# Turning the gated activations by 32 x 32 VectorE transposes and SBUF to SBUF transfers instead of on TensorE

## The chip, the cores and the metric

The kernel runs on one core of a Trainium2 chip. The metric is the device time of one execution in microseconds (us), as a median over runs. The core has five engines that run their own instruction streams in order and meet only through semaphores: TensorE (PE), which multiplies and turns matrices, VectorE (DVE), ScalarE (ACT), GpSimd (POOL) and SyncE (SP), which here issues the weight loads. A transfer can be issued from SP, from ACT or from POOL; the issue is an instruction in that engine's stream.

## The reference

Two transformer blocks in sequence over 256 tokens of width 1024, all in float32. The first has differential attention, retention and a squared-relu feed-forward of width 4096. The second has two gated feed-forwards ("f1" and "f2") of width 2816, one ahead of its attention and one behind it. Only these two are touched:

```
def swiglu(x, w_gate, w_up, w_down):
    return (jax.nn.silu(x @ w_gate) * (x @ w_up)) @ w_down
...
        x = x + FFN_RES * swiglu(rms_norm_2(x, ffn1_norm[l]), ffn1_w_gate[l], ffn1_w_up[l], ffn1_w_down[l])
...
        x = x + FFN_RES * swiglu(rms_norm_2(x, ffn2_norm[l]), ffn2_w_gate[l], ffn2_w_up[l], ffn2_w_down[l])
```

## The kernel before, in words

Weights come from HBM in units of 128 x 2048 float32 (1 MB), issued by SP into six `raw` slots. Every product is made of three: each weight is cut into a high part `w_hi` (ACT, a rounding copy, function `hi`) and a low part `w_lo` (DVE, a subtraction, `lo`, written over the raw slot), and each activation likewise into a `hi` and a `lo` tile. TensorE adds hi by hi, hi by lo and lo by hi.

A gated feed-forward (`gated`, one function of that name per engine) walks over 11 blocks of 256 columns of the 2816, numbered 0 to 10. A step i takes three weight units: v and v+1 hold gate and up columns of block i, v+2 holds the down rows of block i-1. On TensorE the step is: `ff_up` with unit v for both halves of the tokens (tb 0 and 1); `ff_turn`, four 128 x 128 transposes that turn the activation of block i-1 from tokens by columns to columns by tokens, into PSUM; `ff_up` with unit v+1; then `down`, 24 matmuls that multiply the turned block i-1 by unit v+2. Block 0 is done ahead of step 1, steps 2 to 9 stand in a loop of two rounds over four, step 10 is written out behind it with the turns of block 10.

ACT in a step: `hi(v+3)`, two `split` copies of the turned block from PSUM into `fT_hi`, `hi(v+4)`, `silu` for both token halves, `hi(v+5)`. DVE in a step: `lo(v+3)`, two `split` subtractions into `fT_lo`, `lo(v+4)`, two `multiply` (silu times up, into `act_f`), `lo(v+5)`. `hi(u)` waits until unit u-4 is used (four `w_hi` slots), `lo(u)` waits for `hi(u)`, `silu` for its half of `ff_up`, `multiply` for `silu`, `ff_turn` for `multiply`, and `down` for the `split`. The order of each engine's instructions is the order in which the code is written; no scheduler moves them.

Of the kernel before, what the change touches and what calls it, by code (L numbers as in the profile page):

```python
# [28 lines left out]
P = 128  # L29
D, TB, SEQ = 1024, 2, 256  # L30
# [5 lines left out]
HALF = 512  # L36
# [60 lines left out]
def work_batches():  # L97

    order = [("mix", 0, 0), ("mix", 1, 0), ("mix", 0, 1), ("mix", 1, 1)]
    for k in range(IN_CB):  # L100
        if k == 1:
            order += [("qk", 0, tb) for tb in range(TB)]
        if 6 <= k < 14:
            order += [("a", k - 6), ("v", k - 6)]
        if k == IN_CB - 1:
            order += [("ya", 0, 0)]
        if 12 <= k:
            order += [("rv", k - 12)]
    order += [("ya", 0, 1)]
    order += [("ya", 1, h) for h in range(2)]  # L110
    order += [("yr", tb, h) for tb in range(TB) for h in range(2)]
    order += [("m", tb, h) for tb in range(TB) for h in range(2)]
    order += [("mlp", tb, h) for tb in range(TB) for h in range(2)]
    order += [("p",)]
    order += [("ff", 0, tb) for tb in range(TB)]
    order += [("ple", tb, h) for tb in range(TB) for h in range(2)]
    order += [("ffn1", tb, h) for tb in range(TB) for h in range(2)]
    order += [("f1", i, tb) for i in range(FF2 // SUB) for tb in range(TB)]
    order += [("mix2", tb, h) for tb in range(TB) for h in range(2)]
    order += [("mq", tb) for tb in range(TB)] + [("cq", 0), ("cq", 1), ("ckv",)] + [("mk", tb) for tb in range(TB)]  # L120
    for kind in "bl":
        for j in range(BH // 2):
            order += [(kind + "a", 2 * j), (kind + "a", 2 * j + 1)]
            order += [(kind + "v", j)]
    order += [("ffn2", tb, h) for tb in range(TB) for h in range(2)]
    order += [("f2", i, tb) for i in range(FF2 // SUB) for tb in range(TB)]
    return {name: n for n, name in enumerate(order)}
# [38 lines left out]


# [17 lines left out]
def two_blocks(nc, x_d, p_d, g_mix, w_in, lam_q1, lam_k1, lam_q2, lam_k2, g_diff, g_ret, w_bd, w_br, w_out,  # L185
# [85 lines left out]
    fT, pT, fE = [fT0, fT1], [pT0, pT1], [fE0, fE1]  # L271
    (mix_t,) = lay(named["va"], ("mix_t", [P, TB, D]))
# [66 lines left out]
    f_hi, f_ready = sem("f_hi"), sem("f_ready")  # L339
    up_done, act_ready, up_out = sem("up_done"), sem("act_ready"), sem("up_out")  # L340
# [160 lines left out]
    def _(pe):  # L501
# [302 lines left out]
        def ff_up(u, name, i, steps, cols, du=0, di=0):  # L804

            for j in range(2):
# [7 lines left out]
                if j == 0:  # L814
                    ff_turn(name, i - 1, 2 * steps, cols, di)
# [97 lines left out]
        def gated(name, norm, base):  # L913
# [5 lines left out]
            def down(v, i, tb, r=0, first=False, last=False):  # L919

                turned((name, i, tb), 4 * r)
# [13 lines left out]
            with pe.Fori(0, 2) as r:  # L935
# [5 lines left out]
            narrow_block(up(0)[:, :], None, v, 0, HALF, lambda: ff_turn(name, i - 1, 2 * (base + i), SUB))\  # L941
                .then_inc(up_done, 1)
# [8 lines left out]
            else:  # L951
                turned((name, i - 1, 1))
# [165 lines left out]
    def _(act):  # L1118
# [268 lines left out]
        def gated(name, norm, base):  # L1387
# [6 lines left out]

            silu(0, 0)
# [3 lines left out]
            def step(i, r=0):  # L1399
                v = u + 2 + 3 * (i - 1)  # L1400
                hi(v + 3, r)
                for tb in range(TB):
                    split((name, i - 1, tb), 4 * r)
                hi(v + 4, r)
# [8 lines left out]
            for tb in range(TB):  # L1413
                split((name, i - 1, tb))
            hi(v + 3)
            silu(i, 0)
# [141 lines left out]
    def _(vec):  # L1558
# [343 lines left out]
        def gated(name, norm_in, base, norm_out):  # L1902
# [8 lines left out]

            multiply(0, 0)
# [423 lines left out]
```

## Time and profile before

| | |
|---|---|
| median of three runs | 988.9 us (988.61 to 989.17) |
| the profiled execution's own time | 988.44 us |
| its span in the profile | 986.6 us |
| granted TensorE clock | 1.00 of full speed |
| busy share of PE, PEld, DVE, ACT, POOL | 99, 83, 60, 51, 7 per cent |
| span of the two gated feed-forwards | about 507 to 676 us and about 808 to 977 us |

The span is the time from the first to the last instruction on the core. PE is the matmul side of TensorE, PEld its weight loads (of the stationary operand), which run beside it. Busy shares count neither the issuing of transfers nor waits.

### The profile page before, as it was taken

The page shows a single profiled execution, that of the slowest core. Times are in us where ns is not written, and L with a number is a line of the kernel's source. Part 1 is how long each engine was busy: PE and PEld are TensorE (multiplying, and loading weights), DVE is VectorE, ACT ScalarE, POOL GpSimd, SP SyncE. Part 2 cuts the span into 40 slices and gives each one's busy share as a digit, 9 for nine tenths or more (in the row PEclk, how much of TensorE's full clock was granted, in tenths as well). Part 3 has the DMA queues.
Part 4 walks back from the last instruction along what each step waited for, and adds up shares of the span by engine and source line. Part 5 has one row for each costly group of instructions (what it writes and reads, how often), then busy time and mean ns, then how long its engine had stood idle before and what let it go on. Part 6 is the DMA issues. An engine that isn't in the chain of part 4 may idle for free.

```text
span 986.6 us, 13371 instructions
## 1 busy us (share of the span) xinstructions
PE 979.5 (99%) x5000; PEld 822.5 (83%) x5000; DVE 594.9 (60%) x847; ACT 499.8 (51%) x707; POOL 65.9 (7%) x97
## 2 busy tenths in 40 slices
PE   9999999999999999999999999999999999999997
PEld 7989888888889888888888888888887788888886
DVE  6646655478666555665775545446658875455544
ACT  7444555744365444444684444435648674343433
POOL 4101000020020000000120000000203020000000
PEclk9999999999999999999999999999999999999999
DMA  9754554434465655555566555544654256556531
GB/s 344 254 178 164 171 171 162 154 129 171 171 220 202 195 189 191 193 185 167 177 212 206 178 186 197 174 145 135 217 177 145 86 173 194 189 177 206 172 126 43
DMA packets 98726, 175.71 MB, mean 178 GB/s; under 512 B 5920, under 2 KB 54128, under 8 KB 98672
## 3 DMA queue, kind: packets, MB, share of 16 engines
q1 hardware_dynamic: 97024, 171.53, 51.6%
q0 software_dynamic: 1344, 3.19, 1.2%
q8 instruction: 35, 0.57, 0.2%
q10 hardware_dynamic: 304, 0.27, 0.1%
q14 instruction: 19, 0.16, 0.0%
HBM read 173.91 MB, written 1.05 MB: 177 GB/s over the span
## 4 chain that ended last, share of the span: by engine, by line
PE 99%; issue 0%; DVE 0%; ACT 0%; POOL 0%; POOLq 0%; ACTq 0%
PE bank L523 76%; PE bank L644 6%; PE bank L857 5%; PE bank L537 4%; PE bank L862 2%; PE bank L836 1%; PE bank L582 1%; PE bank L581 1%; PE bank L593 1%; PE bank L994 1%; PE bank L678 0%; PE bank L1056 0%; PE bank L595 0%; PE bank L594 0%; PE bank L613 0%
## 5 line engine op out<-in xcount | busy, mean ns | idle before, releaser
L1573 DVE TENSOR_TENSOR w_lo<-raw,w_hi 128x2048 fp32r<-128x2048 f32 (+1 forms) x159 | 359.3, 2265 | 222.6 <-ACT w_hi L1131 222.4
L523 PE MATMUL bank<-w_hi,hA 128*128 128x512 f32 (+1 forms) x1368 | 431.5, 392 | 0.0
L1131 ACT ACTIVATE w_hi<-raw 128x2048 fp32r<-128x2048 f32 (+1 forms) x162 | 306.0, 1893 | 178.0 <-PE bank L523 133.1
L523 PEld LDWEIGHTS bank<-w_hi,hA 128*128 128x128 f32 x1368 | 255.4, 188 | 51.5 <-issue 0.6
L523 PE MATMUL bank<-w_lo,hA 128*128 128x512 f32 (+1 forms) x684 | 259.8, 387 | 0.0
L523 PEld LDWEIGHTS bank<-w_lo,hA 128*128 128x128 f32 x684 | 128.6, 188 | 25.0
L523 PE MATMUL bank<-w_hi,fT_hi 128*128 128x512 f32 x232 | 71.8, 391 | 0.0
L523 PE MATMUL bank<-w_hi,fT_lo 128*128 128x512 f32 x232 | 71.5, 389 | 0.0
L523 PE MATMUL bank<-w_lo,fT_hi 128*128 128x512 f32 x232 | 71.5, 389 | 0.0
L1138 ACT ACTIVATE fT_hi<-bank 128x256 fp32r<-128x256 f32 (+1 forms) x46 | 15.9, 391 | 86.2 <-PE bank L537 86.2
L644 PE MATMUL bank<-hA,w_hi 128*128 128x256 f32 x320 | 58.2, 284 | 0.0
L857 PE MATMUL bank<-hA,w_hi 128*128 128x512 f32 x192 | 52.3, 394 | 0.0
L523 PEld LDWEIGHTS bank<-w_lo,fT_hi 128*128 128x128 f32 x232 | 43.5, 188 | 9.2
L523 PEld LDWEIGHTS bank<-w_hi,fT_lo 128*128 128x128 f32 x232 | 43.5, 188 | 9.1
L644 PEld LDWEIGHTS bank<-hA,w_hi 128*128 128x128 f32 x320 | 49.8, 192 | 0.6 <-ACT va L1183 0.3
L523 PEld LDWEIGHTS bank<-w_hi,fT_hi 128*128 128x128 f32 x232 | 43.0, 188 | 8.7 <-issue 0.2
L2190 POOL TENSOR_SCALAR ms<-ss 128x1 f32<-128x1 f32 x15 | 9.4, 626 | 609.0 <-ACT junk L1161 608.7
L1392 ACT ACTIVATE act_r<-bank,rs 128x256 f32<-128x256 f32 x44 | 20.9, 475 | 53.9 <-PE bank L523 52.2
L1592 DVE TENSOR_TENSOR fT_lo<-bank,fT_hi 128x256 fp32r<-128x256 f32 (+1 forms) x46 | 18.1, 432 | 45.1 <-ACT fT_hi L1138 45.1
L644 PE MATMUL bank<-hA,w_lo 128*128 128x256 f32 x160 | 45.3, 283 | 0.0
L857 PEld LDWEIGHTS bank<-hA,w_hi 128*128 128x128 f32 x192 | 33.2, 189 | 4.8
L1600 DVE SCALAR_TENSOR_TENSOR hA<-bank,g_col,hA 128x128 fp32r<-128x128 f32 x92 | 25.3, 343 | 16.6 <-ACT hA L1143 16.4
(306 smaller groups left out, 1086.0 us busy)
## 6 DMA issues: line engine op xcount, KB each, us to landing
raw<-in_w_in SPq DMA_DIRECT2D x74, 512.0 KB, 4.5
raw<-in_w_ff SPq DMA_DIRECT2D x64, 512.0 KB, 4.3
raw<-in_ffn_w_gate SPq DMA_DIRECT2D x44, 512.0 KB, 3.8
raw<-in_ffn_w_up SPq DMA_DIRECT2D x44, 512.0 KB, 4.8
raw<-in_ffn_w_down SPq DMA_DIRECT2D x44, 512.0 KB, 4.0
raw<-in_w_out SPq DMA_DIRECT2D x16, 512.0 KB, 4.2
raw<-in_w_branch_diff SPq DMA_DIRECT2D x8, 512.0 KB, 4.3
raw<-in_w_branch_ret SPq DMA_DIRECT2D x8, 512.0 KB, 4.3
```

The lines of the kernel that those rows point to most:

```text
L523: mm = pe.matmul(o, a, w, start=first and t == 0 and m < len(outs), stop=last and t == n - 1 and m >= len(todo) - len(outs))
L537: mm = pe.transpose(work(name)[0:cols, col:col + rows], blk, ident)
L581: pe.matmul(b[:, 0:P], q[:, h, 0:P], k[:, h, 0:P], start=True, stop=True)
L644: mm = pe.matmul(out, w, a[:, kt, :], start=(j, f % 2, t, m) == (0, 0, 0, 0), stop=(j, t, m) == (1, 3, 2), skip_group_check=True)
L857: pe.matmul(out[:, :], hi, hA_both[:, kt, :, :], start=(j, t) == (0, 0), stop=(j, t) == (1, 3), skip_group_check=True)
L862: mm = pe.matmul(out[:, 0:SEQ], lo, hA[0][:, kt, :], start=False, stop=(j, t) == (1, 3), skip_group_check=True)
L1131: act.activation(w_hi[u % HI_SLOTS][:, 0:w], raw[u % RAW_SLOTS][:, 0:w], ACT.Copy).then_inc(hi_ready, 1)
L1138: act.activation(dst, b, ACT.Copy).then_inc(split_hi, 1)
L1392: act.activation(act_r[:, tb, 0:SUB], up(tb, i)[:, 0:SUB], ACT.Silu, scale=inv_rms(norm, tb))\
L1573: vec.tensor_tensor(w_lo[u % RAW_SLOTS][:, 0:w], raw[u % RAW_SLOTS][:, 0:w], w_hi[u % HI_SLOTS][:, 0:w].bitcast(f32), ALU.subtract).then_i ...
L1592: vec.tensor_tensor(dst, b, hi.bitcast(f32), ALU.subtract).then_inc(work_out[WB[name] % 2], 1)
L1600: vec.scalar_tensor_tensor(out=dst[:, n, :], in0=b[:, n, :], scalar=g_col[:, c0 + n:c0 + n + 1], in1=hi[:, n, :].bitcast(f32), op0=ALU.mul ...
```

## The change

Blocks 1 to 9 of both gated feed-forwards are no longer turned on TensorE. DVE turns each token half of `act_f` in squares of 32 x 32 into a tile `act_Q` (`turn_act`, two instructions). ACT then issues sixteen transfers from `act_Q` to `act_T` (`carry`), each 32 partitions by 128 columns (16 KB), which put the squares into the right groups of partitions. `turned_split` (ACT) copies `act_T` into `fT_hi` in one instruction of 128 x 512, `turned_low` (DVE) writes `fT_lo` in one of the same size, where there were two of 128 x 256 each. Blocks 0 and 10 stay as they were.

```
@@ ff_up
-                if j == 0:
+                if j == 0 and i == 1:
                     ff_turn(name, i - 1, 2 * steps, cols, di)
@@ gated, TensorE
-                turned((name, i, tb), 4 * r)
+                if i in (0, n - 1):
+                    turned((name, i, tb))
+                else:
+                    pe.wait_ge(turned_lo, TURNED[name] + i + 4 * r)
...
-            narrow_block(up(0)[:, :], None, v, 0, HALF, lambda: ff_turn(name, i - 1, 2 * (base + i), SUB))\
-                .then_inc(up_done, 1)
+            narrow_block(up(0)[:, :], None, v, 0, HALF).then_inc(up_done, 1)
@@ gated, ScalarE
+            def carry(i, r=0):
+
+                act.wait_ge(act_turned, 2 * (TURNED[name] + i + 4 * r))
+                for a in range(4):
+                    for j in range(4):
+                        act.dma_start(act_T[32 * j:32 * j + 32, a, :], act_Q[32 * a:32 * a + 32, j, :]).then_inc(act_moved, 16)
+
+            def turned_split(i, r=0):
+                act.wait_ge(act_moved, 256 * (TURNED[name] + i + 4 * r))
+                act.activation(fT[0][:, 2 * (i % 2):2 * (i % 2) + 2, :].rearrange("p k (t a c) -> p a (k t) c", a=4, c=32),
+                               act_T[:, :, :].rearrange("p a (n c) -> p a n c", c=32), ACT.Copy).then_inc(turned_hi, 1)
...
-                hi(v + 3, r)
-                for tb in range(TB):
-                    split((name, i - 1, tb), 4 * r)
-                hi(v + 4, r)
+                if i == 1:
+                    hi(v + 3, r)
+                    for tb in range(TB):
+                        split((name, 0, tb))
+                    hi(v + 4, r)
+                else:
+                    carry(i - 1, r)
+                    hi(v + 3, r)
+                    hi(v + 4, r)
+                    turned_split(i - 1, r)
...
-            for tb in range(TB):
-                split((name, i - 1, tb))
+            carry(i - 1)
             hi(v + 3)
+            turned_split(i - 1)
             silu(i, 0)
@@ gated, VectorE
+            def turn_act(i, r=0):
+
+                vec.wait_ge(up_out, 2 * (base + i) + 2 + 8 * r)
+                there = act_Q[:, :, :].rearrange("p j (k t c) -> p t j k c", k=2, c=32)
+                for tb in range(TB):
+                    vec.transpose(there[:, tb], act_f[:, tb, 0:SUB].rearrange("p (k j f) -> p j k f", j=4, f=32)).then_inc(act_turned, 1)
+
+            def turned_low(i, r=0):
+
+                vec.wait_ge(turned_hi, TURNED[name] + i + 4 * r)
+                hi, dst = (t[:, 2 * (i % 2):2 * (i % 2) + 2, :] for t in fT)
...
+                if i > 1:
+                    turn_act(i - 1, r)
                 lo(v + 3, 12 * r)
-                for tb in range(TB):
-                    split((name, i - 1, tb), 4 * r)
+                if i == 1:
+                    for tb in range(TB):
+                        split((name, 0, tb))
                 lo(v + 4, 12 * r)
+                if i > 1:
+                    turned_low(i - 1, r)
...
-            for tb in range(TB):
-                split((name, i - 1, tb))
+            turn_act(i - 1)
+            turned_low(i - 1)
+            multiply(i, 0)
             lo(v + 3)
-            multiply(i, 0)
             split((name, i, 0))
```

ScalarE, step 2 of the first feed-forward, before (L1131 is `hi`, L1138 `split`, L1392 `silu`; ISA and REGISTER_ALU compute the loop's wait values; unit_used counts used weight units, up_done finished halves of `ff_up`):

```order
L1131 ACTIVATE w_hi_83<-raw_75 128x2048 [waits raw_in5]
L1135 ISA
L1138 ACTIVATE fT_hi<-bank 128x2x128 [waits work_done]
L1135 REGISTER_ALU
L1138 ACTIVATE fT_hi<-bank 128x2x128 [waits work_done]
L1128 REGISTER_ALU
L1131 ACTIVATE w_hi_84<-raw_70 128x2048 [waits raw_in0,unit_used]
L1306 REGISTER_ALU
L1392 ACTIVATE act_r<-bank,rs 128x256 [waits rstd_ready,up_done]
```

The same place of the change (L1137 is `hi`, L1406 the transfers of `carry`, L1410 `turned_split`, L1398 `silu`; act_turned is counted up by DVE's transposes, act_moved by the landings):

```order
L1406 DMA act_T<-act_Q 32x128 [waits act_turned]
L1406 DMA act_T<-act_Q 32x128 x15
L1134 ISA
L1135 ISA [waits unit_used]
L1137 ACTIVATE w_hi_83<-raw_75 128x2048 [waits raw_in5]
L1134 REGISTER_ALU
L1137 ACTIVATE w_hi_84<-raw_70 128x2048 [waits raw_in0,unit_used]
L1409 REGISTER_ALU
L1410 ACTIVATE fT_hi<-act_T 128x4x4x32 [waits act_moved]
L1312 REGISTER_ALU
L1398 ACTIVATE act_r<-bank,rs 128x256 [waits rstd_ready,up_done]
```

Sixteen issues now stand at the head of the step, ahead of both `hi`, and the copy into `fT_hi` has moved from between the two `hi` to behind them.

VectorE, the same step, before (L1573 is `lo`, L1592 `split`, L1909 `multiply`):

```order
L1573 TENSOR_TENSOR w_lo_81<-raw_75,w_hi_83 128x2048 [waits hi_ready]
L1591 ISA
L1592 TENSOR_TENSOR fT_lo<-bank,fT_hi 128x2x128 [waits split_hi]
L1591 REGISTER_ALU
L1592 TENSOR_TENSOR fT_lo<-bank,fT_hi 128x2x128 [waits split_hi]
L1571 REGISTER_ALU
L1573 TENSOR_TENSOR w_lo_76<-raw_70,w_hi_84 128x2048 [waits hi_ready]
L1908 ISA
L1909 SCALAR_TENSOR_TENSOR act_f<-bank,rs,act_r 128x256 [waits act_ready]
```

And of the change, from the last `lo` of step 1 on (L1597 is `lo`, L1941 `turn_act`, L1948 `turned_low`, L1933 `multiply`):

```order
L1597 TENSOR_TENSOR w_lo_80<-raw_74,w_hi_82 128x2048 [waits hi_ready]
L1970 UNCONDITIONAL_BRANCH
L1970 ISA
L1941 STREAM_TRANSPOSE act_Q<-act_f 128x8x32 [waits up_out]
L1941 STREAM_TRANSPOSE act_Q<-act_f 128x8x32
L1595 ISA
L1597 TENSOR_TENSOR w_lo_81<-raw_75,w_hi_83 128x2048 [waits hi_ready]
L1595 REGISTER_ALU
L1597 TENSOR_TENSOR w_lo_76<-raw_70,w_hi_84 128x2048 [waits hi_ready]
L1945 ISA
L1948 TENSOR_TENSOR fT_lo<-act_T,fT_hi 128x4x4x32 [waits turned_hi]
```

The transposes stand behind the last `lo` of the step before, and the subtraction into `fT_lo` stands behind both `lo` of its own step. On TensorE the rows of the step are the same but for the four transposes, which are gone; `down` waits for turned_lo, that is, for `turned_low` of the whole block, where it waited for each token half apart.

## Rows read from the trace of the kernel before

**Rows 1.** The page: busy times, and the chain that ended last, by engine.

```profile
PE 979.5 (99%) x5000; PEld 822.5 (83%) x5000; DVE 594.9 (60%) x847; ACT 499.8 (51%) x707; POOL 65.9 (7%) x97
...
PE 99%; issue 0%; DVE 0%; ACT 0%; POOL 0%; POOLq 0%; ACTq 0%
```

**Rows 2.** Windows, step 2 of f1: stretch, length, PE, PEld, DVE, ACT, POOL, clock, DMA share.

```profile
527.80:544.60 16.80, 16.80 (x79) 13.91 (x77) 8.51 (x7) 7.13 (x7) 0.00 (x0) 1.00 0.57 188
```

**Rows 3.** Timeline, PE in step 3: start, length, engine, line, tile.

```profile
543.96 0.39 PE L523 MATMUL bank<-w_hi,hA 128*128 128x512 f32 x1
...
544.19 0.60 PE L537 MATMUL bank<-masks,act_f 128*128 128x128 f32 x4
...
544.86 0.40 PE L523 MATMUL bank<-w_lo,hA 128*128 128x512 f32 x1
...
550.12 0.62 PE L523 MATMUL bank<-w_hi,fT_hi 128*128 128x512 f32 x2
...
555.56 0.39 PE L523 MATMUL bank<-w_hi,hA 128*128 128x512 f32 x1
```

**Rows 4.** Timeline, ACT at the end of step 3.

```profile
550.32 0.47 ACT L1392 ACTIVATE act_r<-bank,rs 128x256 f32<-128x256 f32 x1 [2.25 <-PE bank L523]
550.69 1.91 ACT L1131 ACTIVATE w_hi<-raw 128x2048 fp32r<-128x2048 f32 x1
```

**Rows 5.** Timeline, DVE in steps 1 and 3.

```profile
511.33 4.50 DVE L1573 TENSOR_TENSOR w_lo<-raw,w_hi 128x2048 fp32r<-128x2048 f32 x2 [1.32 <-ACT w_hi L1131]
515.75 0.75 DVE L1592 TENSOR_TENSOR fT_lo<-bank,fT_hi 128x256 fp32r<-128x256 f32 x2
...
518.61 0.87 DVE L1909 SCALAR_TENSOR_TENSOR act_f<-bank,rs,act_r 128x256 f32<-128x256 f32 x2
519.39 2.28 DVE L1573 TENSOR_TENSOR w_lo<-raw,w_hi 128x2048 fp32r<-128x2048 f32 x1
...
552.63 2.29 DVE L1573 TENSOR_TENSOR w_lo<-raw,w_hi 128x2048 fp32r<-128x2048 f32 x1 [1.32 <-ACT w_hi L1131]
```

**Rows 6.** Tiles: 128 x 512 from SBUF on ACT and DVE; a 128 x 256 cast.

```profile
L1323 ACT ACTIVATE fT_hi<-act_f x6: 625/631/637, 333.4 to 422.5; 128x512 fp32r<-128x512 f32 x6
L1847 DVE TENSOR_TENSOR fT_lo<-act_f,fT_hi x6: 684/685/687, 335.8 to 424.9; 128x512 fp32r<-128x512 f32 x6
...
689.16 0.28 DVE L1995 CAST pos_k<-pos_ki 128x256 f32<-128x256 int32 x1
```

**Rows 7.** Timeline, transfer issues of ACT and SP at the start.

```profile
1.21 0.57 ACTq L1218 DMA_DIRECT2D g_rows<-in_g_mix  x1
...
1.18 0.90 SPq L402 DMA_DIRECT2D raw<-in_w_in  x2
2.12 0.43 SPq L395 DMA_DIRECT2D x<-in_x  x1
2.60 0.91 SPq L402 DMA_DIRECT2D raw<-in_w_in  x2
3.54 0.43 SPq L395 DMA_DIRECT2D x<-in_x  x1
4.02 0.43 SPq L402 DMA_DIRECT2D raw<-in_w_in  x1
```

**Rows 8.** Source L376, SP's weight issues: ns least, median, most.

```profile
L376 SPq DMA_DIRECT2D raw<-in_ffn_w_down x44: 328/345/647, 490.7 to 947.2; - x44
```

**Rows 9.** DMA issues: KB each, median us from issue to landing.

```profile
raw<-in_ffn_w_up SPq DMA_DIRECT2D x44, 512.0 KB, 4.8
...
out<-src ACTq DMA_DIRECT2D x1, 192.0 KB, 2.6
...
lam_v<-in_lam_k POOLq DMA_DIRECT2D x2, 32.0 KB, 6.1
```

**Rows 10.** Timeline, PE at `down` of block 1.

```profile
533.30 0.62 PE L523 MATMUL bank<-w_hi,fT_hi 128*128 128x512 f32 x2
```

More of the change, by code:

```diff
@@ L117, in work_batches @@
     order += [("ffn1", tb, h) for tb in range(TB) for h in range(2)]
-    order += [("f1", i, tb) for i in range(FF2 // SUB) for tb in range(TB)]
+    order += [("f1", i, tb) for i in (0, FF2 // SUB - 1) for tb in range(TB)]
     order += [("mix2", tb, h) for tb in range(TB) for h in range(2)]
@@ L125, in work_batches @@
     order += [("ffn2", tb, h) for tb in range(TB) for h in range(2)]
-    order += [("f2", i, tb) for i in range(FF2 // SUB) for tb in range(TB)]
+    order += [("f2", i, tb) for i in (0, FF2 // SUB - 1) for tb in range(TB)]
     return {name: n for n, name in enumerate(order)}
@@ L165 @@
         _n += 1
+TURNED = {"f1": 0, "f2": FF2 // SUB - 2}
 TALL = (1, 2, 3, 6, 7)
@@ L271, in two_blocks @@
     fT, pT, fE = [fT0, fT1], [pT0, pT1], [fE0, fE1]
+    act_Q, act_T = lay(named["fE_lo"] + 16 * SEQ, ("act_Q", [P, 4, P]), ("act_T", [P, 4, P]))
     (mix_t,) = lay(named["va"], ("mix_t", [P, TB, D]))
@@ L339, in two_blocks @@
     f_hi, f_ready = sem("f_hi"), sem("f_ready")
+    act_turned, act_moved, turned_hi, turned_lo = sem("act_turned"), sem("act_moved"), sem("turned_hi"), sem("turned_lo")
     up_done, act_ready, up_out = sem("up_done"), sem("act_ready"), sem("up_out")
@@ L951, in gated @@
             else:
-                turned((name, i - 1, 1))
+                pe.wait_ge(turned_lo, TURNED[name] + i - 1)
                 turned((name, i, 1))
@@ L1910, in multiply @@
                                          in1=act_r[:, tb, 0:SUB], op0=ALU.mult, op1=ALU.mult).then_inc(up_out, 1)
+            def turn_act(i, r=0):
+                vec.wait_ge(up_out, 2 * (base + i) + 2 + 8 * r)
+                there = act_Q[:, :, :].rearrange("p j (k t c) -> p t j k c", k=2, c=32)
+                for tb in range(TB):
+                    vec.transpose(there[:, tb], act_f[:, tb, 0:SUB].rearrange("p (k j f) -> p j k f", j=4, f=32))                       .then_inc(act_turned, 1)
+            def turned_low(i, r=0):
+                vec.wait_ge(turned_hi, TURNED[name] + i + 4 * r)
+                hi, dst = (t[:, 2 * (i % 2):2 * (i % 2) + 2, :] for t in fT)
+                there = "p k (t a c) -> p a (k t) c"
+                vec.tensor_tensor(dst.rearrange(there, a=4, c=32), act_T[:, :, :].rearrange("p a (n c) -> p a n c", c=32),
+                                  hi.bitcast(f32).rearrange(there, a=4, c=32), ALU.subtract).then_inc(turned_lo, 1)
             multiply(0, 0)
```

## The prediction

> **What bounds the kernel now.** I read the page first. TensorE is busy for 99% of the span and the chain that ended last is 99% PE [rows 1]: whatever is taken out of TensorE's stream shortens the kernel by that much, and whatever makes TensorE wait lengthens it by that much. Then I read a step of a gated feed-forward by windows [rows 2]: it lasts 16.80 us, PE is busy for all of it, DVE for 8.51 and ACT for 7.13. So ACT and DVE look half idle. But those shares hide two things: transfer issues are not in them, and the two engines work in turns with TensorE. The timeline shows where the turns lie [rows 3, 4, 5].
>
> **What is taken out of TensorE.** Matmuls of 512 columns start every 0.227 us: `down` begins at 550.12 and the next step at 555.56, 5.44 us for 24 matmuls [rows 3]. Round the four transposes: the last matmul ahead of them starts at 543.96, the second behind them at 544.86, so 0.90 us for what would be two intervals of 0.227. The transposes cost 0.45 us. A step of 72 matmuls without them is 16.80 - 0.45 = 16.35 us. Nine blocks in two feed-forwards: 18 x 0.45 = **8.1 us** is all that can be won.
>
> **What is put in its place.** One chain must now be done for each block: last `lo` of the step before, two transposes, sixteen issues, `hi(v+3)`, both `lo`, `turned_low`. The order rows show that the issues stand at the head of ACT's step, and that ACT is one in-order stream. Nothing that ACT computes can fill them: the issues wait for DVE's transposes, which stand behind `lo(v+5)`, which waits for ACT's last `hi`; and behind the issues wait both `hi`, for which DVE waits in turn. The prices:
>
> - One issue. The trace has few issues in a row. At the start SP issues from 1.18 to 4.02 six times without a wait, (4.02 - 1.18) / 6 = 0.473 us each [rows 7]. Later single issues take 0.328 us at least and 0.345 in the middle [rows 8]; with the 0.04 that lies between two issues (1.18 + 0.90 to 2.12, [rows 7]) 0.375. Sixteen: 7.5 us by the first, 6.0 by the second. The upper end is 0.55, from ACT's own issue of 0.57 [rows 7]: 8.8 us. I take **7.5 us**, since this is a long row of issues and the first rows are the only rows of that kind; the transfers are smaller than any of those, which speaks for less, so the low end stays in the range.
> - `hi` 1.91 [rows 4]; two `lo` in a row 4.50, two `multiply` 0.87, one `lo` 2.28 [rows 5]; `turned_split` 0.63 and `turned_low` 0.69 from the same sizes out of SBUF [rows 6]. In a row each DVE instruction starts some 0.08 before the end shown of the one ahead (515.75 against 511.33 + 4.50 = 515.83, [rows 5]).
> - The transposes are in no row. Below: a plain 128 x 256 pass, 0.28 each [rows 6]; above, each as long as a whole 128 x 512 pass, 0.69 [rows 6]. The nearest rows are the two 128 x 256 `split` that they stand for, 0.75 for both [rows 5]. I take **0.75**.
>
> The Trainium skill (VectorE: DVE Perf Modes, "The three transpose paths") gives 311 ns for a bfloat16 128 x 128 on VectorE, and a block has four of those: an estimate from that page is 1.24 us, which would make the step 0.5 us longer and the whole some 8 us slower than below. No row here has a VectorE transpose.
>
> **The cycle of ACT and DVE.** From the first issue of one block to the first of the next: 7.5 issues + 1.91 `hi(v+3)` + 4.50 two `lo` + 0.69 `turned_low` + 0.87 two `multiply` + 2.28 `lo(v+5)` + 0.75 transposes = 18.5, less four overlaps of 0.08, plus two handovers of about 0.05: **18.3 us**. A second cycle goes through TensorE and spans two steps. From the end of `ff_up` (550.12) `silu` starts after 0.20 and `hi(v+5)` after 0.37 more [rows 3, 4]; then 1.91, `lo` 2.29, transposes 0.75, issues 7.5, `hi` 1.91, two `lo` 4.50, `turned_low` 0.69: 20.1 us until the `down` of this block can start, which is one step on. From that start TensorE has 16.35 us of work to the end of `ff_up` of the step behind it. Together 36.5 for two steps, 18.2 each. Both say about 18.3, against 16.80 now. TensorE would then wait 18.3 - 16.35 = 2.0 us ahead of every `down`, for `turned_low`, which stands behind both `lo`. A step costs **1.5 us** more.
>
> **The sum for one feed-forward.** Step 2 starts the lag. In the trace the last `lo` of step 1 ends at 519.39 + 2.28 = 521.7 [rows 5]; transposes to 522.4; issues to 529.9; `hi` to 531.9; two `lo` and `turned_low` to 537.0. TensorE started this `down` at 533.30 [rows 10]: **3.7 us** late. Steps 3 to 9: 7 x 1.5 = **10.5**. Step 10 is written otherwise. Counted from the start of the `down` before: DVE's two `multiply`, `lo` and transposes 3.8, issues 7.5, landing of the last transfer about 2.6 [rows 9], `turned_split` 0.63, `turned_low` 0.69, `multiply` 0.48: 15.7. TensorE comes to the transposes of block 10 after the rest of `down` and three runs of 12 matmuls, 5.44 + 3 x 2.72 (12 x 0.227) = 13.6. It waits 2.1, less the 0.45 of transposes gone: **1.6**. The feed-forward is 15.8 us longer, both 31.6 us. The profiled execution would be 988.44 + 31.6 = 1020.0, its span 1018.2, and the median, 0.5 higher, **1020.5**.
>
> **Landing.** The last transfer must be in 3.8 us after its issue (two `hi`), if the copy isn't to wait; but later still does no harm on DVE's chain: `hi(v+5)`, which follows the copy and the two `silu`, must end when `lo(v+5)` can start, 1.97 + 4.5 + 0.6 + 0.8 = 7.9 after the last issue, and it needs 0.63 + 0.75 + 1.9 = 3.3 of that. So a landing of up to 4.6 us is covered by the `hi` and `lo` beside it. The nearest rows are 2.6 for ACT's own, 4.8 for the weight halves of 512 KB, 6.1 for 32 KB issued by POOL [rows 9]. The 16 KB pieces come singly, 0.47 apart, so they should land like the first.
>
> **The rivals.**
> 1. *The issues are covered* and the 8.1 us are won. That asks for the second cycle to fit into 16.35 a step: its parts without the issues are 36.5 - 7.5 = 29.0, and 29.0 + issues = 32.7, so 3.7 us for sixteen, 0.23 each. No issue row here is under 0.328 [rows 8]; only cheaper issues of small transfers could do it. Time: 988.9 - 8.1 = **980.8**. Chance 5%. A step as long as before (33.6 for two) comes out at 4.6 us, 0.29 each; within 0.2%: 2%. The Trainium skill (DMA: Bandwidth & Descriptors, "Issuing engines are not separate DMA queues") calls the sequencer's time for a DMA "usually small relative to the DMA itself"; by that alone this rival would be the likely one. Here sixteen of them stand in one stream and add up.
> 2. *The transfers land late.* Weight loads hold the DMA engines for 57% of a step [rows 2]. If small transfers queue behind them and land after 6 us, each step gets 1.4 us more (6 - 4.6), step 10 3.4 more: 2 x (0.2 + 7 x 1.4 + 3.4) = 27 more, **1047**. The rows of 4.8 and 6.1 [rows 9] speak for it, ACT's 2.6 against it. Chance 10%.
> 3. *Cheap issues, but not cheap enough*: 0.375 each. The first cycle is 16.8, the second (29.0 + 6.0) / 2 = 17.5. A step costs 0.7: 2.2 + 4.9 + 0.1 = 7.2 for each feed-forward, **1003**. This is the same mechanism as the forecast and is counted with it.
>
> **How the numbers follow.** Forecast (issues set the cycle) 83%, with its own range 1003 to 1043; the upper end is issues of 0.55: cycle 19.55, step 2.75 more, 5.0 + 19.3 + 2.9 = 27.2 for each, 54 in all. Transposes of 0.28 or 0.7 move it by 3 down or 11 up, inside that. Rival 1 5%, no change 2%, rival 2 10%. The range 1003 to 1043 leaves out rival 1, no change, and most of rival 2. Under 0.2%, 2 us, a measurement of this kernel can't be told from no change: faster 0.05, same 0.02, slower 0.93.
>
> **What the profile would show.** PE in steps 3 to 9 idle about 2 us ahead of the first matmul of `down`, released by DVE's `turned_low`; steps of 18.3 us; ACT's queue issuing for about 7.5 us per block from the end of DVE's transposes on; the copy `turned_split` not waiting for a landing. PE's busy time about 8 us less. Wrong if issues take 0.3 us or less, if the copy is released by the transfers instead, or if PE waits for nothing there.

## The result and the profile after

The changed kernel takes 1072.24 us (median of five runs, 1070.88 to 1074.28) where the kernel before takes 988.61 beside it. The ratio is 1.0847 [1.0832, 1.0861]: 8.5% slower. The forecast had the side right and the size wrong, 1020.5 us with a range up to 1043. Its span in the profile is 1071.2 us, at a mean granted clock of 0.962 of full speed.

The page, with busy times, TensorE's granted clock in 40 slices, the chain that ended last, and the landing of the new transfers:

```profile
PE 1005.2 (94%) x4928; PEld 835.5 (78%) x4928; DVE 599.9 (56%) x865; ACT 493.9 (46%) x689; POOL 65.6 (6%) x97
...
PEclk9999999999999999999988989899999998999889
...
PE 64%; ACTq 16%; issue 10%; DVE 5%; ACT 4%; POOL 0%; DVEq 0%; POOLq 0%
...
act_T<-act_Q ACTq DMA_DIRECT2D x288, 16.0 KB, 2.3
```

The chain was 99% PE [rows 1]. Now 16% of the span is ACT's queue issuing transfers. Another 10% has the tag "issue", time in which the chain finds no wait: the gaps of 0.03 us between two issues are in it, and for the most part stretches in which DVE's `lo` runs (2.03 us from 541.16 on, inside the `lo` that starts at 540.99). The DMA engines aren't in the chain at all. The clock was 1.00 throughout; now slices in both gated feed-forwards show less than nine tenths.

Windows, steps 2 and 3 of f1, from one burst of issues to the next (columns as in [rows 2]):

```profile
522.80:544.00 21.20, 14.25 (x57) 11.31 (x56) 8.76 (x8) 6.75 (x6) 0.00 (x0) 0.82 0.51 162
544.00:565.70 21.70, 19.47 (x76) 15.59 (x75) 8.76 (x8) 6.87 (x6) 0.00 (x0) 0.89 0.49 157
```

A step was 16.80 us with PE full. It is now 21 to 22. DVE and ACT do about what they did, and the mean clock over the stretch is 0.82 and 0.89.

The timeline of ACT over one step:

```profile
522.83 10.23 ACTq L1406 DMA_DIRECT2D act_T<-act_Q  x16
533.25 3.71 ACT L1137 ACTIVATE w_hi<-raw 128x2048 fp32r<-128x2048 f32 x2 [13.87 <-issue]
536.87 0.61 ACT L1410 ACTIVATE fT_hi<-act_T 128x512 fp32r<-128x512 f32 x1
537.38 0.82 ACT L1398 ACTIVATE act_r<-bank,rs 128x256 f32<-128x256 f32 x2
538.10 1.90 ACT L1137 ACTIVATE w_hi<-raw 128x2048 fp32r<-128x2048 f32 x1
```

And of DVE:

```profile
519.83 2.28 DVE L1597 TENSOR_TENSOR w_lo<-raw,w_hi 128x2048 fp32r<-128x2048 f32 x1
522.03 0.76 DVE L1941 STREAM_TRANSPOSE act_Q<-act_f 128x256 f32<-128x256 f32 x2
535.19 4.49 DVE L1597 TENSOR_TENSOR w_lo<-raw,w_hi 128x2048 fp32r<-128x2048 f32 x2 [12.39 <-ACT w_hi L1137]
539.60 0.68 DVE L1948 TENSOR_TENSOR fT_lo<-act_T,fT_hi 128x512 fp32r<-128x512 f32 x1
540.20 0.87 DVE L1933 SCALAR_TENSOR_TENSOR act_f<-bank,rs,act_r 128x256 f32<-128x256 f32 x2
540.99 2.28 DVE L1597 TENSOR_TENSOR w_lo<-raw,w_hi 128x2048 fp32r<-128x2048 f32 x1
543.19 0.76 DVE L1941 STREAM_TRANSPOSE act_Q<-act_f 128x256 f32<-128x256 f32 x2
```

These two lists are one closed ring. The burst starts as the transposes end, DVE then sits for 12.39 us until `hi` is done, runs without a gap to its next transposes, and the next burst starts at 543.99. The ring is 21.16 us: 10.23 of issues and 10.93 of everything else. The prediction had 7.5 and 10.8.

The timeline of PE from the end of `ff_up` into `down`:

```profile
533.08 0.39 PE L527 MATMUL bank<-w_hi,hA 128*128 128x512 f32 x1
540.42 1.22 PE L527 MATMUL bank<-w_hi,fT_hi 128*128 128x512 f32 x2 [6.96 <-DVE fT_lo L1948]
541.43 1.05 PE L527 MATMUL bank<-w_lo,fT_hi 128*128 128x512 f32 x2
...
545.70 0.99 PE L527 MATMUL bank<-w_hi,fT_hi 128*128 128x512 f32 x2
546.53 0.63 PE L527 MATMUL bank<-w_lo,fT_hi 128*128 128x512 f32 x2
547.00 0.62 PE L527 MATMUL bank<-w_hi,fT_lo 128*128 128x512 f32 x2
...
548.82 0.39 PE L527 MATMUL bank<-w_hi,hA 128*128 128x512 f32 x1
```

PE waits 6.96 us for `turned_low`. The matmuls behind that wait start 0.43 us apart, not 0.227: this is the lower of the clock's two levels, 1.2 GHz. From about 546 on they are 0.23 apart again. So this `down` takes 8.40 us (540.42 to 548.82) instead of 5.44, 3.0 more. Over the 16 blocks whose `down` waits, the loss is 1.8 us in the mean: 1.5 to 3.0 in fourteen of them, and only 0.1 behind the two shortest waits (1.65 and 1.72 us). PE's busy time *rose* from 979.5 [rows 1] to 1005.2 though it has 72 transposes less.

The issues by source, who waited for their tile, and PE's wait in the list of waits:

```profile
L1406 ACTq DMA_DIRECT2D act_T<-act_Q x288: 514/612/1481, 522.8 to 1046.4; - x144
...
  ACT fT_hi L1410: 0.2, 1
...
PE bank L527 <- DVE fT_lo L1948: 54.7, 16, 7.0
```

The median issue is 612 ns long. A landing was waited for once in 18 blocks, for 0.2 us. PE's wait ahead of `down` stands 16 times, 54.7 us in all: 3.4 in the mean, 1.65 at least.

### The profile page after: what moved, and what is told of

Its sections match the earlier page's. It is cut to its first block, busy times and chain, and to the rows that moved or that the text cites. A ratio compares the mean times of both kernels' runs of the same rounds, so it can differ in the third digit from the quotient of the medians.

```text
span 1071.2 us, 13467 instructions
## 1 busy us (share of the span) xinstructions
PE 1005.2 (94%) x4928; PEld 835.5 (78%) x4928; DVE 599.9 (56%) x865; ACT 493.9 (46%) x689; POOL 65.6 (6%) x97
## 4 chain that ended last, share of the span: by engine, by line
PE 64%; ACTq 16%; issue 10%; DVE 5%; ACT 4%; POOL 0%; DVEq 0%; POOLq 0%
PE bank L527 43%; ACTq L1406 16%; PE bank L648 5%; PE bank L861 4%; ACT w_hi L1137 4%; PE bank L541 3%; PE bank L866 2%; DVE w_lo L1597 1%; DVE act_Q L1941 1%; DVE act_f L1933 1%; PE bank L840 1%; DVE fT_lo L1948 1%; PE bank L586 1%; PE bank L585 1%; PE bank L1000 0%
## 5 line engine op out<-in xcount | busy, mean ns | idle before, releaser
L1597 DVE TENSOR_TENSOR w_lo<-raw,w_hi 128x2048 fp32r<-128x2048 f32 (+1 forms) x159 | 357.6, 2262 | 331.0 <-ACT w_hi L1137 330.9
L1137 ACT ACTIVATE w_hi<-raw 128x2048 fp32r<-128x2048 f32 (+1 forms) x162 | 304.1, 1891 | 381.9 <-issue 211.6
L527 PE MATMUL bank<-w_hi,fT_hi 128*128 128x512 f32 x232 | 85.4, 454 | 54.7 <-DVE fT_lo L1948 54.7
L527 PEld LDWEIGHTS bank<-w_hi,fT_hi 128*128 128x128 f32 x232 | 48.6, 219 | 71.0 <-DVE w_lo L1597 61.4
L527 PE MATMUL bank<-w_lo,fT_hi 128*128 128x512 f32 x232 | 81.3, 435 | 0.0
L527 PE MATMUL bank<-w_hi,fT_lo 128*128 128x512 f32 x232 | 79.9, 429 | 0.0
L527 PEld LDWEIGHTS bank<-w_lo,fT_hi 128*128 128x128 f32 x232 | 50.4, 217 | 12.2
L527 PEld LDWEIGHTS bank<-w_hi,fT_lo 128*128 128x128 f32 x232 | 49.7, 214 | 11.8
L1149 ACT ACTIVATE hA<-bank,g_col 128x128 fp32r<-128x128 f32 x92 | 25.5, 379 | 17.1 <-PE bank L541 16.8
L866 PEld LDWEIGHTS bank<-hA,w_lo 128*128 128x128 f32 x192 | 29.4, 189 | 4.0
L648 PEld LDWEIGHTS bank<-hA,w_lo 128*128 128x128 f32 x160 | 30.7, 192 | 0.0
```

Of the source, the lines that this page charges most:

```text
L527: mm = pe.matmul(o, a, w, start=first and t == 0 and m < len(outs), stop=last and t == n - 1 and m >= len(todo) - len(outs))
L648: mm = pe.matmul(out, w, a[:, kt, :], start=(j, f % 2, t, m) == (0, 0, 0, 0), stop=(j, t, m) == (1, 3, 2), skip_group_check=True)
L866: mm = pe.matmul(out[:, 0:SEQ], lo, hA[0][:, kt, :], start=False, stop=(j, t) == (1, 3), skip_group_check=True)
L1137: act.activation(w_hi[u % HI_SLOTS][:, 0:w], raw[u % RAW_SLOTS][:, 0:w], ACT.Copy).then_inc(hi_ready, 1)
L1149: act.activation(dst[:, n, :], b[:, n, :], ACT.Copy, scale=g_col[:, c0 + n:c0 + n + 1]).then_inc(split_hi, 1)
L1597: vec.tensor_tensor(w_lo[u % RAW_SLOTS][:, 0:w], raw[u % RAW_SLOTS][:, 0:w], w_hi[u % HI_SLOTS][:, 0:w].bitcast(f32), ALU.subtract).then_i ...
```

## The experiments

The theory is the prediction's mechanism: each issue is time of ACT, and the ring of issues, ACT and DVE sets the step. What is off is the price of an issue. Either it depends on the form (32 partitions, 16 KB, short rows), or on where the transfer reads: SBUF here, HBM in every row that the prediction used. One rival is that the lowered clock makes the steps long. Another is that the DMA work or its landing does. Letters for theories in a quoted expectation hold for that quotation alone.

### 1. The price of an issue by itself

A kernel (`b_issue`) of nothing but bursts of eight issues, in twelve forms, first from ACT, then from SP. It computes nothing of the reference.

```
def burst(engine, n, form, dst, s):
    kind, parts, cols, off = form
    for k in range(8):
        col = cols * k
        to = dst[off:off + parts, col:col + cols]
        a = q[0:parts, col:col + cols] if kind == "s" else w_in[0:parts, col:col + cols]
        engine.dma_start(to, a).then_inc(s, 16)
    engine.wait_ge(s, 128)
```

> A kernel that does nothing of the reference: bursts of eight transfers in a row, first from ScalarE, then the same from SyncE, twelve forms each (from SBUF or from HBM; 16, 32, 64 or 128 partitions; rows of 128 B to 2 KB; destination at partition 0 or 32), each burst waited for before the next. In the changed kernel an issue of the 32 x 128 piece takes 0.61 us and 0.03 lie between two, where the rows of before showed 0.33 to 0.43 for transfers of 128 partitions. Theory A, that it is the form of the transfer (32 partitions): 0.61 us here too, in the forms with 32 partitions and from both queues, and 0.35 to 0.43 with 128. Theory B, that it is the source in SBUF: 0.61 in all forms from SBUF, 0.43 from HBM. Theory C, that it is ScalarE's queue, or the load beside it in the kernel: 0.43 or less in all of SyncE's bursts, or in both here, where nothing else runs.

By source, one row for a burst (least, median, most ns). `bq` is in SBUF, `in_w_in` in HBM. The forms are, in order: 32 x 128 from SBUF, 32 x 128 from HBM, 128 x 512 (256 KB) from SBUF, the same from HBM, all by ACT, then 32 x 128 from SBUF and from HBM by SP:

```profile
L211 ACTq DMA_DIRECT2D bt<-bq x8: 515/612/614, 19.9 to 24.3; - x8
...
L211 ACTq DMA_DIRECT2D bt<-in_w_in x8: 338/442/445, 38.0 to 41.2; - x8
...
L211 ACTq DMA_DIRECT2D bt<-bq x8: 473/630/637, 47.7 to 52.2; - x8
...
L211 ACTq DMA_DIRECT2D bt<-in_w_in x8: 352/453/454, 54.9 to 58.2; - x8
...
L211 SPq DMA_DIRECT2D bt<-bq x8: 586/590/592, 91.5 to 95.9; - x8
...
L211 SPq DMA_DIRECT2D bt<-in_w_in x8: 340/422/422, 115.4 to 118.6; - x8
```

Among these transfers into SBUF the source decides, not the form. Reading from SBUF an issue takes 0.61 us on ACT and 0.59 on SP; reading from HBM 0.44 and 0.42, whether 16 KB or 256 KB go. The first of a burst is cheaper. (Form isn't nothing: the weight loads of the kernel before, all 512 KB from HBM, have medians from 0.345 us for the down rows [rows 8] to 0.458 for the up columns.) Start to start the SBUF bursts are (24.3 - 19.9) / 7 = 0.63 apart. The HBM figure with its gap of 0.03 is 0.47, just what the prediction read from its HBM rows. The rows were read rightly, but they were rows of the wrong source.

Every burst here writes into SBUF, so the source alone isn't shown to set the price. The kernel before has three issues that read SBUF and write HBM, the stores of its result. The changed kernel with a single transfer per block (`e_one`, below) has single issues from SBUF to SBUF. The first two rows are of the timeline of before, the third is `e_one` by source:

```profile
983.58 0.35 SPq L472 DMA_DIRECT2D out<-src  x1
...
983.63 0.37 ACTq L1554 DMA_DIRECT2D out<-src  x1
...
L1404 ACTq DMA_DIRECT2D act_T<-act_Q x18: 472/472/535, 522.6 to 950.3; - x18
```

Single for single, by ACT, it is 0.37 us from SBUF to HBM and 0.47 from SBUF to SBUF; the first issue of a burst from HBM to SBUF took 0.32 to 0.40. What is dear in these runs is a transfer with both ends in SBUF. No burst from SBUF to HBM was run.

### 2. One transfer, and eight

`e_one`: one transfer of 128 x 512 in place of the sixteen, which leaves the squares in the groups where the transposes put them:

```
-                for a in range(4):
-                    for j in range(4):
-                        act.dma_start(act_T[32 * j:32 * j + 32, a, :], act_Q[32 * a:32 * a + 32, j, :]).then_inc(act_moved, 16)
+                act.dma_start(act_T[:, :, :], act_Q[:, :, :]).then_inc(act_moved, 16)
...
```

Here and in the next kernel the count of landings that `turned_split` waits for is lowered to match.

> The changed kernel with a single transfer per block, the whole of the turned tile (128 partitions by 512 columns, 256 KB), which leaves the squares unmoved between the groups of partitions. Theory of the issues: one issue is covered, steps are 16.35 us, 988.9 - 8.1 = 981 us. Rival, that the two copies behind both lo and the landing hold TensorE even so: 985 to 1000.

Measured: 980.34 us, ratio 0.9915 [0.9899, 0.9932]. The same bytes move and DVE does the same work, in one issue per block of 0.47 us, and the 8 us of transposes are won whole (8.4 against 988.76 beside it). So the bytes and the landing of one large transfer don't make the loss, and the term of 8.1 us for TensorE's saving stands. Sixteen small pieces could still be dearer for the DMA engines than one large one; experiment 4 has a kernel with all sixteen that loses nothing.

`e_eight`: eight transfers of 32 x 256 each, within their own group of partitions:

```
+                for j in range(4):
+                    for b in range(2):
+                        act.dma_start(act_T[32 * j:32 * j + 32, 2 * b:2 * b + 2, :], act_Q[32 * j:32 * j + 32, 2 * b:2 * b + 2, :]).then_inc(act_moved, 16)
```

> The changed kernel with eight transfers per block instead of sixteen, each of 32 partitions by 256 columns (32 KB), so the same bytes in half the issues; the squares land in the wrong groups of partitions. Theory of the issues: 8 x 0.64 = 5.1 us per block, cycle through TensorE (29.0 + 5.1) / 2 = 17.05 us a step, 0.25 over the 16.80 of before; about 2.4 us per feed-forward over before, 993 us. Rival, that the bytes or the landing set it: stays near 1072. Rival, that an issue costs by its bytes: 1.0 us or more each, near 1050 or over.

Measured: 995.85 us, ratio 1.0077 [1.006, 1.0093], granted clock 0.998. A burst of eight is 5.02 us long. The second cycle of the prediction gives (29.0 + 5.0) / 2 = 17.0 a step, 0.2 over the step of before, and with a dearer step 2 and 10 the 993 expected. Measured, the bursts start 17.2 apart in f1 (522.70 to 660.17 over eight), which is part of the 3 us above that. With 1, 8 and 16 issues the time is 980, 996 and 1072: not a straight line, since at first the issues are paid out of slack.

### 3. Is the lowered clock on the path?

`e_warm`: sixteen idle matmuls that read nothing new stand ahead of each `down` of blocks 1 to 8, so that PE is busy while it waits:

```
+                for _ in range(16 if i > 1 else 0):
+                    pe.matmul(bank[7][:, :], junk[:, 0:P], junk[:, 0:HALF], start=True, stop=True)
                 for tb in range(TB):
```

> The changed kernel with sixteen idle matmuls of 128 x 512 bfloat16 (about 3.6 us) on TensorE ahead of each down of blocks 1 to 8, in the time in which TensorE waits. In the changed kernel the granted clock falls to half for part of each step. Theory of the cycle of ScalarE and VectorE: TensorE is not in it, the steps stay at 21.1 us, and only the ends of the two feed-forwards can gain: 1066 to 1073. Rival, that the lowered clock is a good part of the loss: 1050 or less.

Measured: 1074.61 us, ratio to the kernel before 1.0862 [1.0844, 1.088], mean clock 0.992. It lies just above the expected range and shows no gain. One window of a step:

```profile
545.70:566.90 21.20, 21.20 (x94) 16.07 (x93) 8.76 (x8) 6.76 (x6) 0.00 (x0) 0.98 0.52 162
```

PE is full and at 0.98, and the step is still 21.20 us. So the clock isn't what costs this kernel its time in the steps: the ring of ACT and DVE sets the step, and TensorE's slower matmuls lie in its slack. The slack can be worked out. With 10.2 us of issues the cycle through TensorE needs 29.0 + 10.2 = 39.2 for two steps, the ring 2 x 21.0 = 42.0. The slow matmuls that the first passes through, 1.8 us in the mean and 3.0 at most, about fit.

### 4. Other queues, other places

`e_half_sp`: half of the issues from SP, half from ACT (the loop over SP's steps is unrolled for it):

```
+ON_SP = [(a, j) for a in range(2, 4) for j in range(4)]
+ON_ACT = [(a, j) for a in range(2) for j in range(4)]
...
-                for a in range(4):
-                    for j in range(4):
+                for a, j in ON_ACT:
@@ gated, SyncE
+            def carry(k):
...
+                sp.wait_ge(act_turned, 2 * (TURNED[name] + k))
+                for a, j in ON_SP:
+                    sp.dma_start(act_T[32 * j:32 * j + 32, a, :], act_Q[32 * a:32 * a + 32, j, :]).then_inc(act_moved, 16)
+            for i in range(1, FF2 // SUB):
+                step(i)
+                if i > 2:
+                    carry(i - 2)
```

> The changed kernel with eight of the sixteen transfers issued by ScalarE and eight by SyncE, side by side. If the two queues issue independently, ScalarE's burst is 8 x 0.64 = 5.1 us and the time that of the kernel with eight double transfers, 996 us (990 to 1000). Rival, that both queues share what makes an issue long: bursts of up to 10 us on each, 1040 or more.

Measured: 998.56 us, ratio 1.0092 [1.0077, 1.0108]. The medians of one issue stay at 612 on ACT and 591 on SP while both issue: the two queues don't slow each other.

`e_early`: the transposes one place earlier, ahead of the step's last `lo`, all sixteen issues on ACT:

```
-                if i > 1:
-                    turn_act(i - 1, r)
                 lo(v + 3, 12 * r)
...
                     multiply(i, tb, r)
+                turn_act(i, r)
                 lo(v + 5, 12 * r)
...
```

> The changed kernel with the two VectorE transposes moved from behind the step's last lo to ahead of it; sixteen issues on ScalarE as before. The chain between bursts loses one lo: cycle 10.2 + 1.9 + 4.5 + 0.7 + 0.8 + 0.75 = 18.8 us a step instead of 21.1. Eight steps in each feed-forward at 2.3 less and the lead-in 2.3 less: about 1031 us, 1025 to 1038. Rival, that the chain isn't what sets the step: no change, near 1072.

Measured: 1033.07 us, ratio 1.0449 [1.0433, 1.0465]. The 2.28 us of `lo(v+5)` now lie beside the burst. Bursts start at 539.21, 558.92, 578.30 and 597.29, 19.4 apart, against 18.8 in the expectation.

`e_half_early`: both edits together.

> Both edits: eight transfers from each queue and the transposes ahead of the last lo. From the end of ff_up 2.5 us to the burst, 5.1 issues, 1.9, 4.5, 0.7 = 14.7 us, under TensorE's 16.35, so the whole is hidden: 981 us (979 to 984), faster than before by the transposes taken from TensorE. Rival, that the steps stay over 16.35 because of late loads, of the landing, or because the two queues hinder each other: 985 or more.

Measured: **981.72 us** (981.4 to 982.83), ratio 0.9928 [0.9915, 0.9942], faster than both kernels. Its page, a window of one step, and the two bursts:

```profile
PE 971.7 (99%) x4928; PEld 815.4 (83%) x4928; DVE 605.9 (62%) x865; ACT 500.4 (51%) x689; POOL 66.1 (7%) x97
...
556.30:572.60 16.30, 16.30 (x74) 13.50 (x73) 9.13 (x8) 7.12 (x6) 0.00 (x0) 1.00 0.66 210
...
551.62 5.01 ACTq L1417 DMA_DIRECT2D act_T<-act_Q  x8
...
556.15 5.92 SPq L462 DMA_DIRECT2D act_T<-act_Q  x8
```

The step is 16.30 us, which is the 16.35 that 72 matmuls need, at full clock, and PE has 99% again. The sixteen issues still cost ten microseconds of queue time per block. They now lie beside TensorE's work, in two streams. The same sixteen pieces move as in the changed kernel, so the DMA work of small pieces doesn't make its loss either.

`e_sp`: all sixteen from SP, with the transposes where the change has them, each burst behind the loads of the step two further on:

```
+ON_SP = [(a, j) for a in range(4) for j in range(4)]
+ON_ACT = []
```

> The changed kernel with all sixteen transfers issued by SyncE (its loop over the steps written out, each burst behind the loads of the step two on) and none by ScalarE. Nothing else moved. Theory of the issues: ScalarE's stream is free, but the burst of 16 x 0.63 = 10.1 us still lies on the path: from the end of ff_up 5.7 us to the burst, 10.1, landing 2.0, copy 0.6, low part 0.7 = 19.1, plus 16.35 of TensorE, for two steps: 17.7 us a step against 21.1 now; about 1017 us, 1008 to 1025. Rival, that the order of the two hi and lo behind it, and not the queue that issues, sets it: near 1072. Rival, that SyncE's loads then come late: over 1030.

Measured: 1069.96 us, ratio 1.0809 [1.079, 1.0828]. This missed by 53 us. SP, ACT and DVE in one step:

```profile
564.00 0.82 SPq L382 DMA_DIRECT2D raw<-in_ffn_w_down  x2
564.86 10.72 SPq L462 DMA_DIRECT2D act_T<-act_Q  x16
...
576.78 0.63 ACT L1421 ACTIVATE fT_hi<-act_T 128x512 fp32r<-128x512 f32 x1 [5.42 <-DMA act_T<-act_Q]
...
560.81 0.76 DVE L1950 STREAM_TRANSPOSE act_Q<-act_f 128x256 f32<-128x256 f32 x2
```

The transposes are done at 561.6, but the burst starts at 564.86. SP is in order too: the burst stands behind a load of down rows, which waits until the `down` ahead has freed its slot. So `down`, the load 0.86, the burst 10.7, a landing of 1.2, the copy and `turned_low` follow one another. I had counted the burst from the end of the transposes and forgotten what is queued ahead of it.

`e_sp_ahead`: the same with the burst ahead of that load:

```
                     gate_up(v + j, w_g, w_u, 4 * j, r * (4 * SUB) + i * SUB, turns)
+                if i > 2:
+                    carry(i - 2)
...
@@ the loop over steps
                 step(i)
-                if i > 2:
-                    carry(i - 2)
```

> All sixteen issues from SyncE, as in the run that gave 1070 us, but each burst ahead of the load of the down rows of the step two on instead of behind it. In that run the burst started only at the end of down (564.0 for transposes done at 561.6), because that load waits for the slot that down frees, so down, burst, copy and low part stood in one row of 21.4 us. Theory, that this order was the cause: the burst starts when the transposes end, the steps are 17.7 us if the load is not late, 1017 us; the load, now 10 us later, can hold the last hi of a step, up to 1045. Rival, that ScalarE's and VectorE's own order sets it: stays at 1065 to 1075.

Measured: 1060.3 us, ratio 1.0724 [1.0706, 1.0742]. The burst now follows the transposes at once, but what it moved past is late:

```profile
543.06 10.01 SPq L464 DMA_DIRECT2D act_T<-act_Q  x16
553.12 1.06 SPq L382 DMA_DIRECT2D raw<-in_ffn_w_down  x2
...
563.20 11.23 SPq L464 DMA_DIRECT2D act_T<-act_Q  x16
...
558.25 1.92 ACT L1149 ACTIVATE w_hi<-raw 128x2048 fp32r<-128x2048 f32 x1 [2.61 <-DMA raw<-in_ffn_w_down]
```

`hi(v+5)` waits 2.61 us for down rows whose load stood behind the burst; it does so 16 times, 44.2 us together. The trace closes a ring here that doesn't pass through TensorE: burst 10.0 (from 543.06), the load's two issues, `hi(v+5)` at 558.25, then 1.9 for it, 2.3 for `lo(v+5)` and 0.8 for the transposes, and the next burst at 563.20. That is 20.1 us, where the bursts start 20.6 apart over eight steps of f1. So the late load sets most of the step. 1060 is outside both of the expected bounds (up to 1045 with a late load, 1065 or more for the rival), and this run gave back 10 us of the 53.

### 5. The prediction's own price

`e_hbm`: to see whether the sum holds with the price it was made with, the sixteen pieces are read from a weight in HBM. They have the same shapes and the same targets; the values of blocks 1 to 9 are then others.

```
-  act_Q[32 * a:32 * a + 32, j, :]
+  w_in[32 * a:32 * a + 32, j * P:(j + 1) * P]
```

> The changed kernel with the sixteen transfers per block reading pieces of the same size and shape (32 x 128) from a weight tensor in HBM instead of from the turned tile in SBUF, so the values are not those of the reference; everything else as in the changed kernel. The bursts by themselves gave 0.47 us from start to start for this form from HBM and 0.64 from SBUF. If the price of an issue is the one term of the prediction that was wrong, this kernel has the prediction's price (16 x 0.47 = 7.5 us), its steps of 18.3 us and its time: 1020.5 us (1015 to 1026). Rival, that something else of the change costs the rest (the lowered clock, late loads, the form of the copies): 1035 or more.

Measured: 1039.58 us, ratio 1.0506 [1.0488, 1.0523]. The issues have the forecast price, yet the time is 19 us over the forecast: the rival of the expectation came true. By source, by windows, and PE's timeline ahead of `down`:

```profile
L1406 ACTq DMA_DIRECT2D act_T<-in_w_in x288: 317/443/2018, 522.7 to 1014.5; - x144
...
541.30:562.10 20.80, 20.80 (x90) 17.14 (x89) 9.04 (x8) 7.11 (x6) 0.00 (x0) 0.96 0.51 164
562.10:581.60 19.50, 14.50 (x57) 11.59 (x56) 8.74 (x8) 6.75 (x6) 0.00 (x0) 0.88 0.56 176
...
537.73 1.22 PE L527 MATMUL bank<-w_hi,fT_hi 128*128 128x512 f32 x2 [4.35 <-DVE fT_lo L1948]
```

Here the lowered clock does count. With 7.5 us of issues both cycles were forecast at about 18.2. The one through TensorE passes one `down` in two steps, and the first that waited took 8.00 us (537.73 to 545.73) instead of 5.44. With 2.6 us of slow matmuls on top it is (36.5 + 2.6) / 2 = 19.6 a step. The bursts start 19.6 apart (522.75 to 581.65 over three steps; 19.8 over eight). The nine waits of this kernel cost 1.6 to 3.0 us each, 2.2 in the mean. `e_hbm_warm`: the same kernel with eight idle matmuls ahead of each `down`, edited as in experiment 3.

> The kernel with pieces from HBM (issues of 0.47 us; it gave 1039.6 us against the 1020.5 of the prediction's sum) with eight idle matmuls (1.8 us) on TensorE ahead of each down of blocks 1 to 8. In that kernel the steps alternate between 18.6 and 20.8 us, and the windows show a granted clock of 0.88 and 0.96. Theory: the cycle through TensorE (one half of two steps is TensorE's own 16.35 us) is lengthened by the lowered clock that follows each wait; with the wait filled the clock stays up, and the steps come back to 18.3: 1020 to 1027 us. Rival, that the alternation comes from late landings or loads: stays within 3 us of 1039.6.

Measured: 1025.68 us, ratio 1.0374 [1.0356, 1.0391]. The window of a step:

```profile
541.00:559.30 18.30, 18.13 (x81) 13.94 (x80) 8.53 (x9) 6.87 (x6) 0.00 (x0) 1.00 0.56 179
```

At full clock the bursts are 18.6 apart (541.91 to 597.57 over three), against the 18.3 forecast, and the time is 5 us from 1020.5. The lowered clock was worth 14 us. `e_sp_warm`: `e_sp` with the same eight matmuls.

> The kernel with all issues from SyncE behind the load of the down rows (1070 us; steps of 21.4 us, of which down takes 7.1 where 24 matmuls at full clock take 5.44) with the same eight idle matmuls. Down, two load issues 0.9, burst 10.1, landing 1.2, copy and low part 1.3 stand in one row there: at full clock 18.9 us, so 1028 to 1040 us if the clock stays up. Rival, that the lowered clock hangs on the share of idle time and not on this one wait, so that eight matmuls in a step of 19 or more us don't hold it: 1055 or more.

Measured: 1045.25 us, ratio 1.0569 [1.0552, 1.0587], clock 0.992, bursts 19.5 apart in f1. That is 25 us back: of `e_sp`'s miss of 53 about half was the clock, since the row of `down`, load, burst and copies passes through `down` in every step. The time is still 5 us over the upper end that was expected, as the steps are 19.5 and not 18.9. The other 28 us against the 1017 first expected I put down to the order of SP's queue; that is argued, since each of the two orders tried on SP has a cost of its own, the wait for `down` here and the late load in `e_sp_ahead`.

## Why the prediction was wrong in size

**The step that failed** is the price of an issue: "sixteen: 7.5 us", with an upper end of 8.8. It is 10.2, 0.64 from start to start. All rows under it [rows 7, 8] are transfers from HBM into SBUF. Those of the change go from SBUF to SBUF, 0.61 against 0.44 for the same piece (experiment 1); the trace of before has no such transfer. The rows were said to be the only ones of a long run of issues; that their source differs wasn't seen, and "the transfers are smaller than any of those, which speaks for less" is not borne out: bytes hardly matter. The highest row, 0.57, was the one nearest to the truth and still left out 1.4 us of a burst.

With 10.2 in the same sum: `down` of step 2 is 3.7 + 2.7 = 6.4 us late (PE waits 6.96 there, which is 6.4 and the missing transposes); the ring is 10.2 + 10.8 = 21.0, so a step costs 4.2 more, and seven 29.4; step 10 costs 1.6 + 2.7 = 4.3 (in f1 the `down` before takes 7.15 us, 1.7 more than 5.44, and PE then waits 2.43 for the turns of block 10: 4.1 against a forecast wait of 2.1 + 2.7 = 4.8). Together 40.1 for each feed-forward, 80.2 for both, and a median of 1069.1. Measured 1072.2. The 3 us left are of the size of two things that the sum lacks: over eight steps of f1 the bursts start 21.2 us apart, not 21.0, as a few single issues take 1 us and more (most 1481 ns); and behind the turns of block 10 in f1 slow matmuls cost 1.6 us (707.10 to 711.62, 4.52 us, where before it was 665.01 to 667.98, 2.97).

**The rest, step by step.**
- The transposes: 0.75 taken, 0.76 measured. The Trainium skill (VectorE: DVE Perf Modes, "The three transpose paths") gives 311 ns for bfloat16 128 x 128, from which the estimate for a block was 1.24. The trace doesn't agree with that scaling: the two transposes take 0.76, like the two `split` of 128 x 256 before (0.75, [rows 5]).
- `hi`, `lo`, `turned_low`, `multiply`: 3.71 for two `hi`, 4.49, 0.68 and 0.87, all within 0.15 of the sum's.
- The ring binds, PE's wait is ahead of `down` and released by `turned_low`: right, in all 16 places.
- The landing is covered: right. It is 2.3 us in the median and the one wait for it is 0.2 us. Rival 2 (1047) would have been nearer in time than the forecast, for a cause that isn't there; rivals 1 and 3 fell with the price.
- The Trainium skill (DMA: Bandwidth & Descriptors, "Issuing engines are not separate DMA queues") calls the sequencer's time "usually small relative to the DMA itself". By that rule rival 1 was the likely one. This trace shows the opposite for a burst: 10.2 us of issuing for a landing of 2.3.
- TensorE saves 8.1 us: shown by `e_one` (8.4 us faster) and by the step of 16.30 in `e_half_early`. But "PE's busy time about 8 us less" was wrong: 26 us more, for the clock.

**A second miss that cost little here.** The sum held the clock at 1.00. In the changed kernel fourteen of the sixteen waits ahead of `down` are followed by a stretch at the lower level that costs 1.5 to 3.0 us. In the steps the slack takes it (experiment 3); only the 1.6 us at the end of f1 lie outside. At the price that I had assumed it would have made 14 of the 19 us between 1020.5 and the 1039.6 of `e_hbm`. The other 5 are there at full clock too, in steps of 18.6 instead of 18.3. So even with issues of 7.5 us a block the sum was 19 us too low. For the kernel as it is, where the ring sets the step, the price of the issue is the step that failed.

What stays open: why an issue with both ends in SBUF is dearer, and whether a burst from SBUF to HBM would be.

## What to carry to other kernels

Count a burst of small transfers as work in the issuing engine's in-order stream, at the price of an issue with the same source and target (0.64 us each from SBUF to SBUF here), and ask what stands behind it and what it stands behind. To keep such a burst, split it over two queues and start its chain as early as the data allow: that turned 8.5% slower into 0.7% faster, where moving it whole to the other queue gained almost nothing. And where a change makes TensorE wait in each step, price the matmuls behind the wait at the lower clock in every cycle that passes through them.

## What the runs showed of the hardware

- In a burst into SBUF an issue takes 0.61 us on ACT and 0.59 on SP if the transfer reads SBUF, 0.44 and 0.42 if it reads HBM, and hardly depends on its size (16 and 256 KB). Single issues took 0.47 from SBUF to SBUF (`e_one`) and 0.34 to 0.37 from SBUF to HBM (before). Two engines that issue at once don't slow each other (612 and 591 ns in `e_half_sp`).
- A busy TensorE that waited 4.35 us or 6.96 us ran its next matmuls 0.43 us apart instead of 0.227, for about 5 us. Shorter waits were followed by such a stretch in some cases and not in others: in `e_sp` each of eleven waits of 2.69 to 2.75 us cost 1.5 to 3.0 us, in `e_early` waits of 2.37 us cost 1.7 twice and nothing once, in the changed kernel waits of 1.65 and 1.72 cost nothing. `e_eight` and `e_half_sp`, whose waits are 2.1 us at most, stayed at 0.998 and 0.997. Idle matmuls in the wait kept the mean clock at 0.99 and above; they gave back 14 us (`e_hbm`) and 25 us (`e_sp`), and nothing in the changed kernel, where the ring of ACT and DVE sets the step.
- A VectorE transpose of 128 x 256 float32 in squares of 32 takes 0.38 us.
